# One inference step of a streaming encoder: the token groups of the input projection, 256 and 288 columns instead of 128 and 416

## The reference, cut to what matters

```python
h = _rmsnorm(x, norm1_g)
z = jnp.einsum("btd,de->bte", h, w_in)     # qa ka va qb kb vb f gates
oa, ob = attend(...)                        # diff-attention and FoX attention
merged = gates[:, :, 0] * (oa @ w_pa) + gates[:, :, 1] * (ob @ w_pb)
x = x + merged @ w_o
q = (rmsnorm(x) @ peer_wq)                  # scores, two top-16, top-16 of sums
out = sum over picks of g * gelu(u[e] . xb) * v[e]
```

## Time and profile before

| | |
|---|---|
| median of 3 runs | 2528.22 us |
| lowest and highest | 2521.9 and 2529.8 us |
| the profiled execution | 2525.66 us, of it 2523.9 us span |
| PE matmul busy | 1918.7 us (76%) |
| VectorE busy | 1580.9 us (63%) |
| ScalarE, POOL busy | 516.7 us (20%), 720.6 us (29%) |
| HBM read and written | 744.77 MB and 18.30 MB |
| mean granted TensorE clock | 0.843 of full speed |

### The profile page before, as it was taken

How to read it: one execution, slowest core, us unless ns; L and a number is a source line. 1 busy time by engine, 2 the same in 40 slices (tenths; PEclk the granted TensorE clock), 3 DMA queues, 4 the chain that set the end, 5 groups by cost and what they waited for, 6 DMA issues and landing times. The chain is left out here.

```text
span 2523.9 us, 22586 instructions
## 1 busy us (share of the span) xinstructions
PE 1918.7 (76%) x7276; PEld 1153.4 (46%) x7276; DVE 1580.9 (63%) x3637; ACT 516.7 (20%) x1354; POOL 720.6 (29%) x697
## 2 busy tenths in 40 slices
PE   7989889988495766895776699567765886787755
PEld 6855567556245632343652244456221343683211
DVE  0021112787476588868869785777975656649956
ACT  2221201111251101542110153211012331101111
POOL 0000000144133233334324432424442214224442
PEclk9998899999687897977898897779886766658878
DMA  7832365499779987879998977899998568978887
GB/s 249 285 115 80 99 211 197 184 421 421 272 277 376 355 323 281 321 269 385 421 416 351 366 288 266 329 416 416 377 352 311 220 231 305 378 297 320 320 330 294
DMA packets 139301, 764.98 MB, mean 303 GB/s; under 512 B 18608, under 2 KB 42464, under 8 KB 52016
## 3 DMA queue, kind: packets, MB, share of 16 engines
q0 software_dynamic: 78336, 570.46, 57.5%
q1 hardware_dynamic: 24912, 154.73, 16.6%
q10 hardware_dynamic: 35936, 38.35, 4.6%
HBM read 744.77 MB, written 18.30 MB: 302 GB/s over the span
## 5 line engine op out<-in xcount | busy, mean ns | idle before, releaser
L615 POOL DMA_INDIRECT ring<-in_uv,stage x544 | 668.0, 1228 | 1272.5 <-DVE vsum L1554 412.4
L1206 PE MATMUL acc<-ring,diag 128*128 128x512 f32 (+1 forms) x1152 | 649.3, 716 | 248.5 <-DVE diag L1540 248.5
L1529 DVE CUSTOM_DVE_ANT_0 ring<-ring,xb 128x1024 f32<-128x1024 f32 x544 | 648.4, 1219 | 123.4 <-DMA ring<-in_uv,stage 103.4
L1206 PEld LDWEIGHTS acc<-ring,diag 128*128 128x128 f32 (+1 forms) x1152 | 243.5, 222 | 611.9 <-DVE diag L1540 330.2
L1554 DVE SCALAR_TENSOR_TENSOR vsum<-ring,coefd,vsum 128x1024 f32<-128x1024 f32 x251 | 322.5, 1285 | 9.1 <-DVE coefd L1547 0.2
L887 ACT ACTIVATE gel<-dots 128x1 f32<-128x1 f32 x544 | 103.3, 201 | 1024.5 <-DVE dots L1529 1007.2
L985 PE MATMUL pz<-F,wbuf 128*128 128x416 f32 (+1 forms) x656 | 244.4, 532 | 7.2 <-ACT kaT L743 2.5
L633 POOL COPY stage<-idx 128x4 int32<-128x4 int32 x136 | 49.8, 366 | 502.0 <-DVE gw L1485 482.3
L985 PEld LDWEIGHTS pz<-F,wbuf 128*128 128x128 f32 (+1 forms) x656 | 127.0, 196 | 118.0 <-issue 118.0
L1540 DVE TENSOR_SCALAR diag<-ident,gel,gw 128x128 f32<-128x128 f32 x268 | 93.2, 352 | 104.7 <-ACT gel L887 97.9
L1547 DVE TENSOR_SCALAR coefd<-gel,gw 128x1 f32<-128x1 f32 x256 | 53.4, 209 | 125.1 <-ACT gel L887 124.7
(11 more groups left out here) (310 smaller groups left out, 2135.3 us busy)
## 6 DMA issues: line engine op xcount, KB each, us to landing
wbuf<-in_w_z SPq DMA_DIRECT2D x52, 1024.0 KB, 5.8
wbuf<-in_w_q SPq DMA_DIRECT2D x40, 1024.0 KB, 9.0
wbuf<-in_w_pa SPq DMA_DIRECT2D x20, 1024.0 KB, 9.1
wbuf<-in_w_o SPq DMA_DIRECT2D x20, 1024.0 KB, 9.3
wbuf<-in_w_pb SPq DMA_DIRECT2D x20, 512.0 KB, 7.8
ring<-in_uv,stage POOLq DMA_INDIRECT x544, 8.8
zT<-F ACTq DMA_DIRECT2D x28, 208.0 KB, 3.0
wbuf<-in_w_sk SPq DMA_DIRECT2D x5, 1024.0 KB, 7.4
```

Of the source, the lines that this page charges most:

```text
L615: pool.indirect_dma_start(out=ring[:, slot, :], out_offset=None, in_=d["uv"], in_offset=bass.IndirectOffsetOnAxis(ap=stage[:, a, k:k + 1], ...
L1206: last = nc.tensor.matmul(acc[0:nq, c * 512:(c + 1) * 512], diag[:, parity, 0:nq], ring[:, slot, D + c * 512:D + (c + 1) * 512], start=Fal ...
L1529: nc.vector.tensor_tensor_reduce(out=u, in0=u, in1=xb[:, t % 2, :], scale=1.0, scalar=0.0, op0=ALU.mult, op1=ALU.add, accum_out=dots[:, sl ...
```

## The change

Group 0 becomes tiles 0 and 1 (256 columns), group 1 becomes tiles 2, 3 and the sample (288 columns). Tile 1's norm and transposes move ahead of the first chunk, and with them the load of tile 2's tokens. The buffers for outgoing units get a fixed 512 columns, since a unit of group 1 has 288 and one of group 0 has 2 x 256. Three waits follow: every tile but 0 waits for the last group's saves, the first toeplitz waits for 16 copies instead of 8, and tile 1's transposes no longer wait for the toeplitz copies, which now come after them. A qa, qb, g, ka or kb chunk of group 1 is still two units, of group 0 one. A va or vb chunk is one unit for tiles 0 and 1, and two for tiles (2, 3) and (4), where group 0 had one unit of one tile and group 1 two of two tiles.

```diff
-GROUPS = [(0,), (1, 2, 3, 4)]
+GROUPS = [(0, 1), (2, 3, 4)]
...
-    plan = [("norm_h", 0, 0), ("turn_h", 0, 0), ("lambdas", 0, 0)]
+    plan = [("norm_h", 0, 0), ("turn_h", 0, 0), ("norm_h", 1, 0), ("load_x", 2, 0), ("turn_h", 1, 0), ("lambdas", 0, 0)]
...
-    for t in range(1, TILES):
+    for t in range(2, TILES):
...
-        zstage = F[:, KT * n1:KT * n1 + ZSTAGES * n1].rearrange("p (b n) -> p b n", b=ZSTAGES)
-        f0 = KT * n1 + ZSTAGES * n1
+        zstage = F[:, KT * n1:KT * n1 + ZSTAGES * 512].rearrange("p (b n) -> p b n", b=ZSTAGES)
+        f0 = KT * n1 + ZSTAGES * 512
...
-                    wait_saved(act, group_of(t))
+                    wait_saved(act, len(GROUPS) - 1 if t else 0)
...
-                    pe.wait_ge(h_stored, 8)
+                    pe.wait_ge(h_stored, 8 * 2)
...
+                if t >= 2:
+                    pe.wait_ge(toep_copied, HEADS)
                 if t:
-
-                    pe.wait_ge(toep_copied, HEADS)
                     pe.wait_ge(h_stored, 8 * t)
```

## The result

The kernel after takes 2570.85 us (median of 4 runs, 2565.87 to 2572.97), the kernel before 2525.72 beside it: 45 us more by these medians. The ratio on record is 1.0159, 95% interval 1.0123 to 1.0195. It corresponds to 2530.6 us for the kernel before, which is the median of the larger set of its runs beside the first experiments (2530.54, 17 runs); by it the kernel after is 40 us slower (31 to 49). Forecast were 43.3 us more, and 2569 us for the time. The profiled execution has a span of 2568.9 us against 2523.9.

What follows compares the result with a forecast made beforehand. PE bounds group 0's projection and tile 0's attention, DVE top-k's end, full DMA engines the experts. 89.8 + 7.0 - 4.4 - 39.0 - 7.1 - 3 = +43.3 on 2525.7 gives 2569 us, range 2550 to 2584.

Steps and rivals of the forecast that it cites:

- The pass time: Projection matmuls: a pass every 0.2189 us at 256 columns, 0.2454 at 288, almost in proportion to columns.
- Part 1 and 2: Projection of group 0: longer group +89.8 us; tile 1 normalised before the first chunk +7.0 and -4.4.
- The start: PE's first projection waits for 16 copies instead of 8, behind tile 1's norm: +7.0 us, bounds 5 and 10.
- the forget chunk: In group 0, 3.57 us for 16 passes at 128 columns; growth taken as +2.0 us, between 0 and +3.3.
- The stall behind the bias loads: In group 0, tile 1's norm no longer meets the bias loads: -4.4 us including 0.9 for transposes, at worst 0.
- Part 3: Twelve chunks beside tile 0's attention get shorter, mostly 11.41 to 8.02 us: -39.0 us, bounds 0 and -40.
- the lower clock level: Beside tile 0's attention, chunks begun at this level lose some 10 us in all, left unchanged, give or take 3.
- Part 4: Five chunks beside tile 0's top-k: DVE's 7.08 us wait for ACT goes, -7.1 us, not -17.
- Part 5: Ten chunks beside tile 0's experts: -3 us, not the -34.6 of PE alone, as the DMA engines are full.
- The bytes argument: Experts of tile 0: 55.08 MB at 421 GB/s, bytes unchanged, take the same 130.8 us.
- ACT's waits for PE: Experts of tile 0: ACT waits up to 6.4 us for PE and holds back the next rows' activations; -3 us.
- The rivals that gave back 17 or 34.6 us: Experts of tile 0: half the PE saving comes back, 2555 us, chance 0.10; all of it, 2537 us, chance 0.05.

Runs made afterwards that it cites:

- a1: The kernel after, every group 0 chunk summing only four of eight inner-dimension slices, loads, copies and waits kept: 2478.57 us, 92.3 less than after.
- b5: The kernel before with only tile 1's norm and transposes moved ahead of the first chunk, groups unchanged: group 0's last transposes at 138.46 us instead of 137.20.
- b1: The kernel before, chunks 0 to 11 of group 1 (beside tile 0's attention) summing only four of eight slices: 2467.83 us, 62.7 less.
- b9: The kernel before, ACT taking the exponential of the top-k scores two pieces earlier, ahead of the last chunk's copies: ratio 0.9999.
- b3: The kernel before, last ten chunks of group 1 (beside tile 0's experts) with half their matmuls left out, weights still loaded whole: ratio 1.000.
- b2_top_half: The kernel before, chunks 12 to 16 of group 1 (beside tile 0's top-k) with half their matmuls left out: total 0.7% less, 11 to 25 us.
- b4: The kernel before, last ten chunks of group 1 with half their matmuls left out and half their weights not loaded: ratio 0.9987.
- b10: The kernel before with both the six saves spread behind tile 1's attention pieces and the top-k exponential taken early: ratio 0.993.
- b6: The kernel before, the six saves of keys and values issued one each behind attention pieces 2 to 12 of tile 1: ratio 0.9919.

## Why the prediction was right, point by point

- **The pass time.** 0.2189 us at 256 columns gave 7.47 a chunk, measured 7.44; the interpolated 288 gave 8.02, measured 8.00. Time follows columns, so the change moves work and removes none. Shown by both traces.
- **Part 1 and 2, group 0: +92.4 forecast.** The last transposes went from 137.20 to 228.35, +91.2. The start is 6.4 us later (7.0), the forget chunk 1.75 longer (2.0). The stall behind the bias loads is gone, as forecast. a1 shows that this comes from the longer chunks and not from the new place of the norm: it has the new place with chunks of 3.99 us, and the stall costs 4.15 us there. b5, with chunks of 4.11, keeps 1.3 us of it.
- **Part 3: -39.0.** From the forget chunk to M: 285.7 us before, 248.4 after, -37.3. b1 shows the mechanism. Seven chunks in after are longer than 8.0, by 11.3 us in all, where before had 10.6: the lower clock level cost the same, as assumed. That the two traces land within 2 us of the forecast in this part and the one before is in part luck: seven traces of the same work up to M scatter over 5 us.
- **Part 4: -7.1.** M to G is 54.6 instead of 61.6, -7.0. The size was right, the reason incomplete: in b9, where only the wait goes, M to C fell by 1.5 us and the total by nothing that can be measured, since PE is busy nearly throughout M to C. I had treated parts 4 and 5 as independent terms.
- **Part 5: -3.** G to S went from 181.5 to 178.8, -2.7. The number is right, the reason half wrong, and that 3 came out as 2.7 is luck. I argued that full DMA engines leave the stage at 130.8 us. In fact G to C shrank by 7.1, since PE had been a little above DMA, and C to S grew by 4.4: in the trace of after the longest issue of the saves takes 13.71 us, of before 8.98. The bytes argument holds from G to S, not from G to C: by C after has moved 54.77 MB and before 57.68, and the rest follows behind C. I took -3 for ACT's waits for PE and wrote that the bytes do not change. They did: 73.26 MB from G to S instead of 74.41, both at 410 GB/s, which is 2.8 us. After G SP issues six loads of projection weights instead of seven, as one more is issued before it. The rivals that gave back 17 or 34.6 us are excluded by after's own G to S and by b3, whose total stayed within 6 us with half of the matmuls gone.
- **Behind S:** 1856.8 us against 1855.8, nothing.
- The sum of the measured steps is 91.2 - 37.3 - 7.0 - 2.7 + 1.0 = 45.2, the spans differ by 45.0 (the rest is rounding). The forget chunk's start after the last transposes is the same to 0.01 us in both.

What stays open: why b2_top_half gained 11 to 25 us when its trace has 9.1 between M and S, while b4, b9 and b10 (beside b6) are 7.5, 4.1 and 5.9 us shorter there and their totals show less or none of it. The forecast's 43.3 lies between the two measures of the same change, 40 us by the ratio (31 to 49) and 45 by the medians; the runs can't tell them apart.

## What to carry to other kernels

When matmul time follows the columns, rebalancing groups is a transfer between stages: add the columns where the engine works alone and they cost in full, take them where something else is as slow and they come back in part (here 91 us paid, 47 got back). A stall seen on one engine need not be worth its length when another engine is busy through the whole stretch; look at the stretch from where the engines last met to where they meet again. And count the bytes over the stretch up to the next point where the transfers have to have landed, not to where the work on them was issued.

## What was not expected of the hardware

The issue of a DMA from ACT can take long: the 2 MB save of va held ACT's queue for 8.98 us in before, 5.92 in b9_exp_early, 13.71 in after and 13.33 in b4_late_half_bytes. Full DMA engines alone don't do it. In before the saves of ka and kb, issued just ahead of it, took 0.40 and 0.60 us, with the engines as full (a share of 1.01 and 419 GB/s from 625.8 to 637 us). In b6_save_spread the same save of va, issued 12.7 us behind the one before it, took 0.38 us, with the engines at a share of 1.01 and 417 GB/s around it. What differs is that in the block two large saves from the same queue stand right ahead of it; that this is the cause fits all these traces and was not tested. With the saves spread, tile 1's first score came 21 to 29 us after C instead of 40 to 49.
